# Stick-breaking attention: PSUM banks of the scores and of the transposed weights, three and two in place of two and three

## The chip, the cores and the metric

The kernel runs on one core of a Trainium2 chip. The metric is device time in microseconds, the median of several executions. The chip's engines are called as in the profile: PE (TensorE: PE for the matmuls, PEld for its weight loads), DVE (VectorE), ACT (ScalarE), POOL (GpSimd) and SP (SyncE, which here issues most of the transfers). Engines run on their own instruction streams, each in order, and wait for each other by semaphores. Matmuls write PSUM, which has eight banks of 128 x 512 float32; POOL works on SBUF alone in this kernel.

## The reference

One decoder layer over 2048 tokens of width 1024 with two groups of eight heads. Its parts: an adaptive RMS norm of x, one input projection, stick-breaking attention (group A, 64 wide), latent attention with a causal softmax (group B), gates, one output projection and a gated residual. The change is in group A alone:

```python
z = jnp.einsum('bhqd,bhkd->bhqk', qi, k).astype(jnp.float32) * inv_sqrt_d
strict = key_pos[None, :] < q_pos[:, None]
log_keep = jnp.where(strict, jax.nn.log_sigmoid(-z), 0.0)
after = lax.cumsum(log_keep, axis=3, reverse=True) - log_keep
w = jnp.where(strict, jnp.exp(jax.nn.log_sigmoid(z) + after), 0.0)
return jnp.einsum('bhqk,bhkd->bhqd', w.astype(v.dtype), v)
```

In words: each key takes a share of the stick that the later keys have left, so that the weight of a key is the difference of two neighbouring running products of sigmoid(-z), taken from the last key down.

## The kernel before

The kernel has five stages, one after the other: `features` and `tokens` (norm and projections), `attend_sb` (group A), `attend_mla` (group B) and `output`. The stage of group A runs from 836 us to 1320 us of the profiled execution, and the diff touches only it.

**Units and turns.** The stage goes over four pairs of heads, and within a pair over head 0 and head 1. The program of one pair is written out as a list (class `Plan`): 80 units and 80 turns. It is run once as straight code and then three times as the body of a loop, on every engine (`pairs`). So there are 320 units and 320 turns in all; below they are numbered 0 to 319, and turn 157, for example, is turn 77 of the second pair.

- A *unit* is one tile of scores: 128 queries against up to 512 keys. PE makes it by two matmuls (high and low part of q) and a third with the mask where the diagonal lies in it (L1734, L1737), into one of the banks z. ACT takes sigmoid(-z) from the bank into one of four buffers kp (L1574; `KEEPS = 4`, so it waits until DVE has used the unit four back). DVE turns it into the running product by a scan (L1651) and writes the row w.
- A *turn* brings 128 keys of a group of up to four query blocks, already scanned, into the form that the product with the values needs. PE transposes up to four 128 x 128 tiles into one of the banks pt (L1763). Three turns of four are *pooled* (`x % 4` is 0, 1 or 2): ACT copies the bank to SBUF (wf, L1585), which frees the bank; POOL rounds it (wh, L1546) and takes the rest (wl, L1548). The fourth (`x % 4` is 3) is not: ACT writes wh from the bank (L1590), and DVE takes wl from the same bank (L1660), so the bank is free only when DVE has done that.
- The *product* of a turn is two matmuls with the values (L1778, L1779), three turns later on PE (`LAG = 3`). It waits until the turn's wl is there: from POOL for pooled turns, from DVE for the others.
- At the end of each group of turns ACT and DVE add up, gate and split the result (L1598, L1670, L1677, L1610, L1689).

**The order.** All engines follow the same list. PE issues unit n + 1 and then the slot of n, which holds mostly one turn, sometimes none or two; each turn is followed by the product of the turn three back:

```python
unit(it, 0)
for n in range(U):
    if n + 1 < U:
        unit(it, n + 1)
    slot(it, turns_after(n, start))
```

ACT and DVE go unit n, then the slot of n. The turns begin at slot 21 of the first pair, since a group's rows must be scanned before it is turned, and so run into the next pair: turns 57 to 79 of a pair stand in slots 0 to 21 of the next one, and after the fourth pair 23 of them are left (`plan.rest`).

**Banks.** Two banks z, three banks pt (`PTS = 3`), two po for the products and one, `beside`, that holds zeros for the scan: eight. Unit n goes to bank n % 2 and waits until ACT has read unit n - 2 (`reached(pe, s_keep, it * U + n - 1)`). Turn x goes to bank x % 3 and waits until the turn that last used the bank has left it (`bank_before`, `bank_free`): ACT's copy for a pooled one, DVE's subtraction for the other kind. Since 80 is not a multiple of 3, turns 0 and 1 of a pair come only two turns after the last users of their banks.

## Time and profile before

| | us |
|---|---|
| median of 3 runs (lowest, highest) | 2053.9 (2050.63, 2054.33) |
| the profiled execution | 2051.65 |
| its span | 2050.0 |
| stage of group A | 836 to 1320 |
| its first rounding on POOL, its last subtraction there | 861.9, 1316.6 |

Over the whole span PE is busy 92%, its weight loads 75%, DVE 60%, POOL 50% and ACT 46%, and the granted TensorE clock is 0.958 of full speed on average. These shares are means over five stages with different limits, so for this change they say little: the stage itself has to be read, and in it what each engine waits for. A row of the timeline gives start, duration, engine, line, operation and tiles, and in brackets how long the engine had been idle and what ended that. The chain of work that ended last lies in the output stage and doesn't reach back to this one.

### The profile page before, as it was taken

To read this page: it belongs to the slowest core of one execution; us is meant where nothing else is said; L and a number is where in the kernel's file an instruction comes from. 1 tells how busy PE (TensorE), PEld (TensorE's weight loads), DVE (VectorE), ACT (ScalarE), POOL (GpSimd) and SP (SyncE) were. 2 spreads that over 40 slices of the span, in tenths; PEclk is the share of its full clock that TensorE was granted. 3 is DMA by queue.
4 is the path that set the end of the run, shared out by engine and by line. 5 is a ranking of instruction groups with operands and counts; after the bars stand their busy time and mean duration, and the time that the engine had idled before them with its cause. 6 is when DMAs were issued, how large, how long until landed. Compare 5 with 4: busy or idle time off the path is not lost. (4 is left out here: it accounts for less than half of the span.)

```text
span 2050.0 us, 32093 instructions
## 1 busy us (share of the span) xinstructions
PE 1880.1 (92%) x9669; PEld 1537.6 (75%) x9669; DVE 1236.6 (60%) x1864; ACT 948.1 (46%) x1890; POOL 1031.3 (50%) x1044
## 2 busy tenths in 40 slices
PE   6899999979999996599998989599999999997998
PEld 2687888859999985377777777468788887875776
DVE  1642222134555555699989899378988889873110
ACT  1431111133333332377777767457777777771000
POOL 2510000002333343199998989757878778781212
PEclk9899999989999997799999999779999999998999
DMA  7497532334555553731618052244153542605564
GB/s 267 135 320 223 174 112 77 129 145 143 177 200 184 178 177 131 177 82 39 169 37 188 24 152 59 69 101 83 38 125 75 134 82 57 170 21 174 174 195 143
DMA packets 224767, 273.75 MB, mean 134 GB/s; under 512 B 13936, under 2 KB 161680, under 8 KB 219264
## 3 DMA queue, kind: packets, MB, share of 16 engines
q1 hardware_dynamic: 220736, 265.53, 45.5%
q10 hardware_dynamic: 3904, 6.82, 1.1%
q8 instruction: 44, 0.72, 0.2%
q14 instruction: 83, 0.68, 0.1%
HBM read 159.06 MB, written 109.05 MB: 131 GB/s over the span
## 5 line engine op out<-in xcount | busy, mean ns | idle before, releaser
L2039 POOL TENSOR_TENSOR mla_wl<-mla_w,mla_wh 128x512 fp32r<-128x512 f32 (+1 forms) x320 | 379.2, 1200 | 112.8 <-ACT mla_wh L2075 107.0
L1548 POOL TENSOR_TENSOR sb_wl<-sb_wf,sb_wh 128x512 fp32r<-128x512 f32 (+2 forms) x240 | 285.5, 1189 | 19.2
L1651 DVE TENSOR_TENSOR_SCAN sb_w<-sb_kp,sb_w,sb_beside 128x512 f32<-128x512 f32 x192 | 245.5, 1278 | 28.0 <-ACT sb_kp L1574 12.5
L2074 ACT ACTIVATE mla_w<-mla_zt 128x512 f32<-128x512 f32 (+1 forms) x320 | 170.9, 534 | 114.0 <-PE mla_zt L2225 57.2
L2116 DVE TENSOR_REDUCE mla_nmx<-mla_zn 128x1 f32<-128x512 f32 (+2 forms) x320 | 191.3, 600 | 6.0 <-PE mla_zn L2195 3.1
L602 PE MATMUL pt_po<-h_hi,pt_wh 128*128 128x512 f32 x448 | 177.2, 396 | 9.7 <-issue 6.8
L1574 ACT ACTIVATE sb_kp<-sb_z 128x512 f32<-128x512 f32 (+3 forms) x320 | 168.8, 531 | 32.4 <-PE sb_z L1737 12.2
L1585 ACT ACTIVATE sb_wf<-sb_pt 128x512 f32<-128x512 f32 (+2 forms) x240 | 133.3, 555 | 108.3 <-PE sb_pt L1763 105.4
L1763 PE MATMUL sb_pt<-sb_ident,sb_w 128*128 128x128 f32 x1088 | 175.7, 277 | 7.3 <-DVE sb_wl L1660 6.9
L604 PE MATMUL pt_po<-h_hi,pt_wl 128*128 128x512 f32 x448 | 179.2, 400 | 0.0
L603 PE MATMUL pt_po<-h_lo,pt_wh 128*128 128x512 f32 x448 | 177.6, 396 | 0.0
L1546 POOL CAST sb_wh<-sb_wf 128x512 fp32r<-128x512 f32 (+2 forms) x240 | 143.6, 599 | 57.0 <-ACT sb_wf L1585 52.3
L2075 ACT ACTIVATE mla_wh<-mla_zt 128x512 fp32r<-128x512 f32 (+1 forms) x320 | 169.1, 529 | 0.0
L1778 PE MATMUL sb_po<-sb_wh,values 128*128 128x512 f32 (+1 forms) x320 | 145.1, 453 | 20.1 <-POOL sb_wl L1548 19.6
L1734 PE MATMUL sb_z<-keys,q_hi 128*128 128x512 f32 (+3 forms) x320 | 129.9, 406 | 34.0 <-DMA q_lo<-qk_sb 19.5
L1763 PEld LDWEIGHTS sb_pt<-sb_ident,sb_w 128*128 128x128 f32 x1088 | 130.6, 142 | 40.1 <-DVE sb_wl L1660 13.9
L83 POOL MEMSET tk_ident<- 128x128 f32 x1 | 0.2, 204 | 306.3 <-POOLq L62 306.3
L2195 PE MATMUL mla_zn<-keys,q_hi 96*128 96x512 f32 (+2 forms) x320 | 129.1, 409 | 24.8 <-DVE mla_nmx L2116 12.9
L2381 PE MATMUL out_po<-out_wh,out_ms 128*128 128x512 f32 x512 | 137.9, 391 | 6.0 <-DMA out_ms<-mix_mla 6.0
L2142 DVE TENSOR_TENSOR mla_pa<-mla_pa,mla_w 128x512 f32<-128x512 f32 x168 | 116.8, 695 | 30.9 <-ACT mla_w L2074 27.4
L2225 PE MATMUL mla_zt<-q_hi,keys 97*128 97x512 f32 (+1 forms) x320 | 125.9, 393 | 0.1
L2241 PE MATMUL mla_po<-mla_wh,values 128*128 128x512 f32 (+1 forms) x320 | 123.8, 387 | 1.4 <-POOL mla_wl L2039 1.4
(241 smaller groups left out, 4371.6 us busy)
## 6 DMA issues: line engine op xcount, KB each, us to landing
qk_mla<-tk_th SPq DMA_DIRECT2D x64, 192.0 KB, 2.1
qk_mla<-tk_tl SPq DMA_DIRECT2D x64, 192.0 KB, 2.3
whole<-in_w_ada SPq DMA_DIRECT2D x4, 2048.0 KB, 18.5
pt_w<-in_w_feat SPq DMA_DIRECT2D x16, 512.0 KB, 6.0
qk_sb<-pt_oh SPq DMA_DIRECT2D x32, 256.0 KB, 3.4
qk_sb<-pt_ol SPq DMA_DIRECT2D x32, 256.0 KB, 4.1
hT<-h_hi SPq DMA_DIRECT2D x16, 512.0 KB, 5.1
hT<-h_lo SPq DMA_DIRECT2D x16, 512.0 KB, 6.2
```

What stands on the lines that cost most here:

```text
L602: nc.tensor.matmul(bank[:], wh[s][:, k, :], hh[:, k, cols_q], start=(k == 0), stop=False)
L603: nc.tensor.matmul(bank[:], wh[s][:, k, :], hl[:, k, cols_q], start=False, stop=False)
L604: mm = nc.tensor.matmul(bank[:], wl[s][:, k, :], hh[:, k, cols_q], start=False, stop=(k == KD - 1))
L1548: nc.gpsimd.tensor_tensor(wl[i][:, lo:GW], wf[i][:, lo:GW], wh[i][:, lo:GW].bitcast(F32), ALU.subtract).then_inc(s_plo, 1)
L1574: nc.scalar.activation(kp[n % KEEPS][:, 0:width], z[n % 2][:, 0:width], ACT.Sigmoid, scale=-SB_SCALE).then_inc(s_keep, 1)
L1651: nc.vector.tensor_tensor_scan(kept, keeps, beside[:, 0:b - a], 1.0 if u["n"] == 0 else w[u["g"]][:, u["r"], b:b + 1], ALU.mult, ALU.bypas ...
L1763: tp = nc.tensor.transpose(pt[x % PTS][:, r * P:(r + 1) * P], w[tn["g"]][:, r, tn["j"] * P:(tn["j"] + 1) * P], ident[:])
L1778: nc.tensor.matmul(out, vj, wh[x % RING][:, lo:GW], start=tn["first"], stop=False)
L2039: nc.gpsimd.tensor_tensor(wl[i][:, cols], w[i][:, cols], wh[i][:, cols].bitcast(F32), ALU.subtract).then_inc(s_lo, 1)
L2074: nc.scalar.activation(w[i][:, cols], zt[x % 2][:, cols], ACT.Exp).then_inc(s_w, 1)
L2075: nc.scalar.activation(wh[i][:, cols], zt[x % 2][:, cols], ACT.Exp).then_inc(s_wh, 1)
L2116: nc.vector.tensor_reduce(nmx[pc["n"] % 2][:, pc["r"], pc["c"]:pc["c"] + 1], zn[p % 2][:, 0:pc["width"]], AX.X, ALU.max, negate=True).then ...
```

## The change

The stage's eight PSUM banks are shared out anew: three for the scores (`ZS = 3`) and two for the transposed weights (`PTS = 2`). Unit n goes to bank n % 3 and waits for ACT's sigmoid of the last unit that used the bank: unit n - 3, and for units 0 and 1 of a pair the unit two before. Turn x goes to bank x % 2 and waits for turn x - 2. No instruction that computes or moves data is added or taken away, and no transfer is moved.

```diff
-    PTS = 3
+    PTS = 2
+    ZS = 3
...
-        z = [m.ps(f"z{i}", [P, GW]) for i in range(2)]
+        z = [m.ps(f"z{i}", [P, GW]) for i in range(ZS)]
...
-                nc.scalar.activation(kp[n % KEEPS][:, 0:width], z[n % 2][:, 0:width], ACT.Sigmoid,
+                nc.scalar.activation(kp[n % KEEPS][:, 0:width], z[n % ZS][:, 0:width], ACT.Sigmoid,
...
+            def scores_before(n):
+
+                return n - ZS if n >= ZS else max(y for y in range(U) if y % ZS == n % ZS) - U
+
...
-                reached(pe, s_keep, it * U + n - 1)
+                reached(pe, s_keep, it * U + scores_before(n) + 1)
                 q = slice(i * P, (i + 1) * P)
-                out = z[n % 2][:, 0:u["z"] - u["a"]]
+                out = z[n % ZS][:, 0:u["z"] - u["a"]]
```

## Rows read from the trace of the kernel before

**Rows 1.** Windows: us, busy of the five engines, granted clock, DMA share, GB/s

```profile
861.90:1317.30 455.40, 419.82 (x2434) 332.55 (x2432) 396.45 (x440) 323.59 (x663) 417.75 (x480) 0.99 0.36 88
```

**Rows 2.** Groups by line, 836 to 1320 us: busy, mean ns, idle before them and its releaser

```profile
L1548 POOL TENSOR_TENSOR sb_wl<-sb_wf,sb_wh 128x512 fp32r<-128x512 f32 (+2 forms) x240 | 285.5, 1189 | 19.2
...
L1546 POOL CAST sb_wh<-sb_wf 128x512 fp32r<-128x512 f32 (+2 forms) x240 | 143.6, 599 | 57.0 <-ACT sb_wf L1585 52.3 <-PE sb_po L1779 4.0
...
L1651 DVE TENSOR_TENSOR_SCAN sb_w<-sb_kp,sb_w,sb_beside 128x512 f32<-128x512 f32 x192 | 245.5, 1278 | 28.0 <-ACT sb_kp L1574 12.5
...
L1660 DVE SCALAR_TENSOR_TENSOR sb_wl<-sb_pt,sb_wh 128x512 fp32r<-128x512 f32 (+1 forms) x80 | 40.8, 510 | 24.1 <-ACT sb_wh L1590 24.1
```

**Rows 3.** Waits, 836 to 1320 us: us in total, times, longest us

```profile
PEld sb_z L1734 <- ACT sb_kp L1574: 43.1, 83, 1.2
...
PE sb_z L1734 <- ACT sb_kp L1574: 12.7, 29, 0.9
...
PEld sb_pt L1763 <- DVE sb_wl L1660: 13.9, 17, 1.9
...
PE sb_pt L1763 <- DVE sb_wl L1660: 6.9, 7, 1.5
...
POOL sb_wh L1546 <- ACT sb_wf L1585: 52.3, 25, 38.6
...
POOL sb_wh L1546 <- PE sb_po L1779: 4.0, 1, 4.0
```

**Rows 4.** Timeline of POOL: the first instruction of the loop's body, third and fourth pair

```profile
1089.76 0.61 POOL L1546 CAST sb_wh<-sb_wf 128x512 fp32r<-128x512 f32 x1 [3.97 <-PE sb_po L1779]
...
1205.94 0.61 POOL L1546 CAST sb_wh<-sb_wf 128x512 fp32r<-128x512 f32 x1 [3.95 <-ACT sb_wf L1585]
```

**Rows 5.** Timeline around turn 157 (PE 1080.54) and the subtraction of turn 155 (DVE)

```profile
1080.54 0.49 PE L1763 MATMUL sb_pt<-sb_ident,sb_w 128*128 128x128 f32 x3
...
1081.14 0.49 ACT L1585 ACTIVATE sb_wf<-sb_pt 128x384 f32<-128x384 f32 x1 [0.37 <-PE sb_pt L1763]
...
1082.65 0.50 POOL L1546 CAST sb_wh<-sb_wf 128x384 fp32r<-128x384 f32 x1
...
1082.88 0.27 DVE L1660 SCALAR_TENSOR_TENSOR sb_wl<-sb_pt,sb_wh 128x128 fp32r<-128x128 f32 x1
...
1083.21 0.44 PE L1763 MATMUL sb_pt<-sb_ident,sb_w 128*128 128x128 f32 x2 [1.47 <-DVE sb_wl L1660]
```

**Rows 6.** Timeline around turn 93 (PE 991.21) and the subtraction of turn 91 (DVE)

```profile
991.21 0.51 PE L1763 MATMUL sb_pt<-sb_ident,sb_w 128*128 128x128 f32 x3
...
993.32 0.67 DVE L1660 SCALAR_TENSOR_TENSOR sb_wl<-sb_pt,sb_wh 128x512 fp32r<-128x512 f32 x1
...
993.40 0.50 POOL L1546 CAST sb_wh<-sb_wf 128x384 fp32r<-128x384 f32 x1
...
995.22 0.40 POOL L1546 CAST sb_wh<-sb_wf 128x256 fp32r<-128x256 f32 x1 [0.23 <-ACT sb_wf L1585]
```

**Rows 7.** Timeline around turn 237 (PE 1196.73) and the subtraction of turn 235 (DVE)

```profile
1196.73 0.49 PE L1763 MATMUL sb_pt<-sb_ident,sb_w 128*128 128x128 f32 x3
...
1198.50 0.27 DVE L1660 SCALAR_TENSOR_TENSOR sb_wl<-sb_pt,sb_wh 128x128 fp32r<-128x128 f32 x1
...
1198.76 0.97 POOL L1546 CAST sb_wh<-sb_wf 128x384 fp32r<-128x384 f32 x1
```

**Rows 8.** Timeline around turn 5 (PE 867.38) and the subtraction of turn 3 (DVE)

```profile
867.38 0.60 PE L1763 MATMUL sb_pt<-sb_ident,sb_w 128*128 128x128 f32 x4
...
867.75 0.67 DVE L1660 SCALAR_TENSOR_TENSOR sb_wl<-sb_pt,sb_wh 128x512 fp32r<-128x512 f32 x1
```

**Rows 9.** Timeline, subtraction of turn 183 (DVE), turn 185 (PE), rounding of turn 188 (POOL)

```profile
1124.46 0.67 DVE L1660 SCALAR_TENSOR_TENSOR sb_wl<-sb_pt,sb_wh 128x512 fp32r<-128x512 f32 x1
...
1124.65 0.49 PE L1763 MATMUL sb_pt<-sb_ident,sb_w 128*128 128x128 f32 x3
...
1129.82 0.61 POOL L1546 CAST sb_wh<-sb_wf 128x512 fp32r<-128x512 f32 x1 [0.30 <-ACT sb_wf L1585]
```

## The prediction

> **What bounds the stage now.** First the windows and the groups by line for the stage of group A, to see which engine has no time to give. From POOL's first rounding to its last subtraction are 455.4 us, and POOL is busy 417.75 of them, 92% [rows 1]; PE stands at 420 and DVE at 396, so no engine is far behind, but PE's time is that of pipelined matmuls and holds much waiting beside it. POOL's two groups add up to 285.5 + 143.6 = 429.1 us, with small overlaps between them [rows 2]. Next the waits. PE's longest is the one for a score bank: 43.1 + 12.7 = 55.8 us in 112 times, behind ACT's sigmoid. The one for a bank pt behind DVE's subtraction is 13.9 + 6.9 = 20.8 us in 24 times. POOL waited 52.3 us for ACT, but 38.6 of that is its start before the first turn; what is left is 13.7 us in 24 times, and 4.0 us once for PE [rows 3]. Two of these are no waits for data: at the first instruction of the loop's body POOL stood 3.97 us in the third pair and 3.95 us in the fourth, although the named releasers are different ones each time [rows 4]. I read that as the price of going back to the head of the loop, and it is the same for either kernel. So while the turns run, POOL waits for others 13.7 + 4.0 - 3.97 - 3.95 = 9.8 us in all. That is the most that any arrangement of banks can give back here; to take time away from PE's score waits is not yet to take it from the stage.
>
> The second thing to see is where DVE stands. Its full scans take 1.28 us each [rows 2], and in the first part of each pair, where turns 57 to 79 of the pair before are done, it has no gaps and runs late: the subtraction of turn 155 comes at 1082.88, and PE has waited 1.47 us for it when it begins turn 158 at 1083.21 [rows 5]. The release itself costs 1083.21 - (1082.88 + 0.27) = 0.06 us.
>
> **The change part by part.** Every instruction stays as it is, with its duration; only two waits of PE move.
>
> *The score wait* now asks for the sigmoid of unit n - 3. The two engines that it lies between are ACT and PE, and nearly all of the 55.8 us go, since the units are over 1 us apart and the 112 waits are 0.5 us on average. But PE only comes earlier to its next wait. Behind a unit stands a turn, which meets the bank pt, and the product, which waits for POOL's subtraction of the turn three back. For the stage the gain counts only where POOL was idle, so it lies between 0 and 9.8 us. Much of the 9.8 lies right after DVE's late stretch or at the start of a pair, where ACT or DVE is late, and not PE's unit. What is left is of the kind of the 0.30 us before turn 188 [rows 9], where POOL waits for a turn that stands on PE behind a product and a unit. I take two such waits, 0.6 us, for each of four pairs: **-2.4 us**.
>
> *The wait for bank pt* now asks for turn x - 2. Where that turn is pooled, ACT's copy frees the bank early enough: it ended 1081.14 + 0.49 = 1081.63 for turn 157, and PE's next turn began 1.58 us after that [rows 5]. Where it is of the kind that DVE finishes (79 times: each turn with x % 4 = 1), it is another matter, because ACT's copy and then DVE's scans come before the subtraction. What queues behind the held turn on PE: its own product of the turn three back, the next unit of scores, the next turns. Who waits for these: ACT for its copy, POOL for ACT's copy, and DVE for the unit's sigmoid. For each pair I take the latest turn and ask when POOL could have it.
>
> - Turn 157 began at 1080.54; ACT's copy ended 1.09 us later. Its bank would have been free at 1083.15 + 0.06 = 1083.21, 2.67 us late. The copy then ends at 1084.30, and POOL's rounding, which began at 1082.65, starts 1.65 us later [rows 5].
> - Turn 93: free at 993.32 + 0.67 + 0.06 = 994.05 against 991.21, 2.84 us late. With the same 1.09 us the copy ends at 995.14, against POOL's 993.40: 1.74 us, less the 0.23 us that POOL was idle before its next tile anyway: 1.5 us [rows 5, 6].
> - Turn 237: free at 1198.83 against 1196.73, 2.1 us late; copy at 1199.92 against 1198.76: 1.16 us [rows 5, 7].
>
> The earlier late turns of the same stretch don't add up with these: DVE's scans go on without a gap, since their sigmoids lie ready, so DVE keeps its times and only the latest turn counts. After it POOL has no idle time in which to catch up until the next pair starts, and the restart of the loop comes after its last tile, whenever that ends. So a delay here stays. Sum 1.65 + 1.5 + 1.16 = 4.3; to each I add 0.2 us for the hand-over from ACT to POOL, an estimate between the 0.06 us of PE's release and the 0.3 us that POOL was idle before turn 188 [rows 5, 9]: **+4.9 us**.
>
> In the first pair turns 5, 9 and 13 are late too; turn 5 would wait until 868.42 + 0.06 and began at 867.38, so 1.1 us [rows 8]. DVE is in its late stretch, but POOL has just started and has tiles in hand: between 0 and 1.1, I take **+0.5 us**.
>
> In the second part of each pair the turns are little late. The worst is turn 185: 1124.46 + 0.67 + 0.06 = 1125.19 against 1124.65, 0.54 us. POOL has tiles in hand there, but PE has two turns in the next slot and comes late to turn 188, for which POOL already waited 0.30 us [rows 9]. Between 0 and 0.54 for each of four pairs; nearer the upper end, because that wait shows no slack: 0.4 each, **+1.6 us**.
>
> Sum: -2.4 + 4.9 + 0.5 + 1.6 = +4.6 us. The profiled execution took 2051.65 us, 2.25 less than the median of the runs; 2051.65 + 4.6 = 2056.25, which on the median's footing is 2053.9 + 4.6 = 2058.5 us.
>
> The Trainium skill speaks against this sum. Its page "Perfetto Trace Analysis" says under "Matmuls" that independent groups of matmuls should rotate through different banks so that the evacuation of one overlaps the next, and under "Optimization Strategy" that a gap repeated on the engine that should be saturated can mean too little PSUM. By that, 112 repeated waits of PE for two score banks call for the third bank, and the result is the first rival below. The trace agrees that the gap is there; whether PE is the engine that should be saturated is what it leaves open, with POOL at 92%.
>
> **The rivals.**
>
> *The third score bank pays (faster).* PE runs a unit ahead, reaches the turns with x % 4 = 1 no earlier than DVE frees them, and POOL never waits. For it: the score wait is PE's largest, over twice its wait for pt. Against it: POOL's whole idle time is 9.8 us, and the late turns above take some. Price: about 7 of the 9.8, with the late turns absorbed: 2047 us. It decides if the held turns reach POOL before its tiles in hand are used up, that is if a turn is late by under about 1 us everywhere.
>
> *Nothing to be measured.* PE catches up within a few slots, as its score waits are gone, and the delays of 1 to 2 us once in a pair are given back: -2 to +2, 2054 us. For it: about 0.5 us saved in every third unit is near what the held turns cost. Against it: POOL has nothing in which to catch up.
>
> *The held turns hold DVE up too (much slower).* Units of scores stand on PE behind the held turn. If their sigmoids come too late, DVE gets gaps, its next subtraction is later still, and the delays add up instead of overlapping. The full lateness would then be paid: 2.67 + 2.84 + 2.1 + 1.1 + 4 x 0.54 = 10.9 us, and more with the other late turns of each stretch: 2065 to 2070 us. It decides from the point where the lateness, 2 to 3 us, is more than the time for which sigmoids lie ready for DVE, which is at most four buffers of kp, some 4 us.
>
> **How the numbers follow.** The mechanism of the sum, +2 to +9 us, has 0.58; that the gain and the loss cancel 0.16; that the third bank pays 0.12; that the delays add up 0.14. Two tenths of a per cent, about what can be told from no change here, are 4.1 us. Of the likeliest case some 0.17 lie below that. So: faster 0.12, the same 0.16 + 0.17 = 0.33, slower 0.41 + 0.14 = 0.55. The range leaves out the greater part of the faster rival below and half of the slowest above: 2051 to 2067 us; the likeliest case's own is 2056 to 2063.
>
> **What the profile would show.** The waits of PE for sb_kp fall from 55.8 us to under 5, or the first step is wrong. Those for DVE's sb_wl before sb_pt rise from 20.8 to 40 to 65 us, and come at turns with x % 4 = 1. POOL's waits for ACT, beside its start and the loop's head, rise from 9.8 us by 3 to 7, most of it one wait of 1 to 2 us late in the first part of each pair; if they fall, the first rival is right. POOL's, DVE's and ACT's busy times stay within 1%. DVE's waits for sb_kp (12.5 us before the full scans [rows 2]) stay; if they double, the last rival is. The stage gets longer by about 5 us, and the other stages don't change. The prediction would be wrong if delays in a pair's first part were given back before its end, or if DVE's scans lost their backlog.

## The result, and the profile after

The changed kernel takes 2071.44 us (median of 4 runs, 2070.62 to 2074.17) where the kernel before takes 2054.07 us beside it (4 runs): +17.4 us, a ratio of 1.0091 with a 95% interval of 1.0073 to 1.0108. The forecast was 2058.5 us with a range to 2067: the direction is right, the size is not. The profiled execution took 2074.17 us.

The page of the changed kernel, its first lines and the busy times:

```profile
span 2072.5 us, 32093 instructions
...
PE 1879.8 (91%) x9669; PEld 1547.5 (75%) x9669; DVE 1236.4 (60%) x1864; ACT 945.8 (46%) x1890; POOL 1026.6 (50%) x1044
```

The window from POOL's first rounding to its last subtraction, changed kernel (columns as in [rows 1]):

```profile
861.60:1337.10 475.50, 414.94 (x2431) 339.37 (x2429) 395.71 (x442) 321.26 (x663) 414.76 (x480) 0.96 0.35 84
```

It is 475.5 us where it was 455.4 [rows 1], and POOL is no busier in it. The spans differ by 22.5 us; all but 2.4 us of that is idle time of the engine that had none to give, in this one stage. The waits say who it waited for; changed kernel, 836 to 1345 us:

```profile
POOL sb_wh L1547 <- ACT sb_wf L1586: 59.5, 29, 38.1
...
DVE sb_w L1652 <- ACT sb_kp L1575: 55.6, 49, 15.3
...
PEld sb_pt L1768 <- DVE sb_wl L1661: 33.3, 42, 2.9
...
PE sb_pt L1768 <- DVE sb_wl L1661: 21.7, 19, 2.5
...
POOL sb_wh L1547 <- issue: 16.0, 2, 8.2
...
PEld sb_z L1739 <- ACT sb_kp L1575: 8.9, 14, 1.2
...
PE sb_z L1739 <- ACT sb_kp L1575: 4.0, 8, 0.7
...
POOL sb_wh L1547 <- PE sb_po L1784: 4.1, 6, 1.4
```

The wait for DVE's subtraction rose from 20.8 to 55.0 us [rows 3], within the forecast 40 to 65. The score wait fell from 55.8 to 12.9 us, and not to the "under 5" of the forecast. POOL's waits beside its start and the loop's head rose from 9.8 to 25.5 us (59.5 - 38.1 for ACT and 4.1 for PE), where 3 to 7 us more were forecast. And two rows were not foreseen: POOL stood 16.0 us in two waits for nothing that the profile shows ("issue"), and DVE waited 55.6 us for ACT's sigmoids, 15.3 of it at its start, where it had waited 33.4 with 14.7 at the start. The second shows in the groups by line, changed kernel:

```profile
L1652 DVE TENSOR_TENSOR_SCAN sb_w<-sb_kp,sb_w,sb_beside 128x512 f32<-128x512 f32 x192 | 245.5, 1278 | 45.5 <-ACT sb_kp L1575 31.2
```

The duration is that of [rows 2], but the 12.5 us behind ACT have become 31.2. Most of that growth is not from held turns, though. The two longest waits are the scans right after the heads of the loop's body, where DVE stands for ACT, ACT for PE and PE for POOL:

```profile
1108.40 1.28 DVE L1652 TENSOR_TENSOR_SCAN sb_w<-sb_kp,sb_w,sb_beside 128x512 f32<-128x512 f32 x1 [5.63 <-ACT sb_kp L1575]
...
1231.64 1.28 DVE L1652 TENSOR_TENSOR_SCAN sb_w<-sb_kp,sb_w,sb_beside 128x512 f32<-128x512 f32 x1 [6.09 <-ACT sb_kp L1575]
```

With the short ones behind them they are 14.6 us. Without them and the start, DVE's waits for sigmoids are 25.7 us, against 18.4 in the kernel before (18.7, less 0.3 at the same places).

**Where the 20 us came in.** I set the starts of POOL's 240 roundings side by side, changed kernel minus kernel before. This is worked out from the two timelines:

```
turn                 0     4     8    68    76    80   108   144   148   156   160   224   228   236   240   318
us later          -0.3  -0.3  +3.1  +3.8  +3.8  +6.2  +6.5  +5.8  +8.5  +8.5 +12.4 +12.6 +15.3 +15.2 +19.5 +19.8
```

There are four steps of 2.3 to 3.4 us (after turns 5, 77, 145 and 225, that is, x = 5, 77, 65, 65) and two of about 4 us at the heads of the loop's body (turns 160 and 240). The stage grew by 20.0 us: 8.1 at the two heads, 11.9 elsewhere.

**A held turn, read closely.** Timeline of the changed kernel around turn 5:

```profile
868.58 0.67 DVE L1661 SCALAR_TENSOR_TENSOR sb_wl<-sb_pt,sb_wh 128x512 fp32r<-128x512 f32 x1
...
869.29 0.66 PE L1768 MATMUL sb_pt<-sb_ident,sb_w 128*128 128x128 f32 x4 [2.47 <-DVE sb_wl L1661]
...
869.99 0.60 ACT L1586 ACTIVATE sb_wf<-sb_pt 128x512 f32<-128x512 f32 x1 [3.28 <-PE sb_pt L1768]
...
870.49 0.59 ACT L1575 ACTIVATE sb_kp<-sb_z 128x512 f32<-128x512 f32 x1
...
870.78 0.61 POOL L1547 CAST sb_wh<-sb_wf 128x512 fp32r<-128x512 f32 x1 [1.41 <-ACT sb_wf L1586]
...
873.83 1.28 DVE L1652 TENSOR_TENSOR_SCAN sb_w<-sb_kp,sb_w,sb_beside 128x512 f32<-128x512 f32 x1 [0.38 <-ACT sb_kp L1575]
```

PE stands 2.47 us for DVE's subtraction, ACT 3.28 us for PE. The scores that ACT reads at 870.49 were done on PE by 866.83 (the matmul at 866.43 lasts 0.40), and the buffer kp that it writes was free at 867.27, when DVE ended the scan of the unit four back. So this sigmoid is 3.2 us late only because it stands behind the copy of turn 5 in ACT's list. DVE still had sigmoids in hand here; its first wait is the 0.38 us at 873.83. What comes later on DVE makes its next subtraction later, and the next turn with it. And PE, when it goes on, goes at half speed. The changed kernel's windows (us, PE, PEld, DVE, ACT, POOL busy, granted clock, DMA share, GB/s):

```profile
866.00:870.00 4.00, 1.53 (x9) 1.03 (x8) 3.90 (x4) 0.72 (x3) 3.21 (x4) 1.00 0.00 0
870.00:872.00 2.00, 2.00 (x11) 1.84 (x10) 1.78 (x3) 1.58 (x4) 1.14 (x2) 0.68 0.00 0
872.00:874.00 2.00, 2.00 (x9) 1.71 (x9) 1.62 (x3) 0.85 (x3) 1.92 (x3) 0.50 0.01 4
```

The granted clock is 1.00 (2.4 GHz) up to the stand and falls to 0.50 (1.2 GHz) behind it: (1 - 0.68) x 2 + (1 - 0.50) x 2 = 1.6 us of PE's time. It does the same for 3.4 us from 973, 1072 and 1195 us, behind the stands at the other three steps (1.93, 2.23 and 2.23 us), and for 10 us after each head. It does not behind two stands of 2.22 and 1.95 us, at turns 65 and 89. In the kernel before it doesn't fall at any of these turns; its falls in this stage, 3.4 us each, are at 1208, 1290 and 1307 us.

**A head of the loop, read closely.** POOL and SP, changed kernel:

```profile
1093.67 0.74 POOL L1549 TENSOR_TENSOR sb_wl<-sb_wf,sb_wh 128x256 fp32r<-128x256 f32 x1
1102.18 0.61 POOL L1547 CAST sb_wh<-sb_wf 128x512 fp32r<-128x512 f32 x1 [7.76 <-issue]
...
1091.88 1.21 SPq L1452 DMA_DIRECT2D keys<-qk_sb  x2
1093.29 1.11 SPq L1452 DMA_DIRECT2D q_hi<-qk_sb  x2
1094.58 1.11 SPq L1452 DMA_DIRECT2D q_lo<-qk_sb  x2
...
1225.42 0.61 POOL L1547 CAST sb_wh<-sb_wf 128x512 fp32r<-128x512 f32 x1 [8.22 <-issue]
```

and the same place in the kernel before:

```profile
1085.04 0.74 POOL L1548 TENSOR_TENSOR sb_wl<-sb_wf,sb_wh 128x256 fp32r<-128x256 f32 x1
...
1085.74 1.21 SPq L1451 DMA_DIRECT2D keys<-qk_sb  x2
```

Before, SP began to issue the six transfers of 256 KB with the next pair's keys and queries 0.04 us before POOL's last tile ended (1085.78), and POOL went on after 3.97 us [rows 4]. After, POOL's last tile ends 8.6 us later. SP issues only 6.1 us later, as its queue goes by DVE's results: in front of the six stands the store of the last group's output. That is 2.5 us ahead of POOL's end, and POOL stands 7.76 us. In that time two packets of the queue "instruction" move. The DMA view of the changed kernel, 1096.4 to 1097.4 and 1099.6 to 1100.2 us:

```profile
q14 instruction: 1, 0.01, 3.2%
...
q14 instruction: 1, 0.01, 5.7%
```

The first of them begins 2.5 us after POOL's last tile (1094.41), the second ends 5.95 us after it; before, these were 0.0 and 2.04 us. The length of the stand goes with the second. I took all sixteen heads of the eight kernels in which the six transfers are issued ahead of POOL's end and within some 3 us of it: the stands range from 3.95 to 8.62 us, but POOL goes on 1.68 to 1.94 us after the second packet's end in every one (1.82 and 1.76 in the changed kernel). I read this as POOL's program behind the jump being fetched through DMA engines that the transfers keep busy; whose program a packet carries, the trace doesn't say.

### The profile page after: what moved, and what is told of

Same layout as the page of the kernel before. It is cut to its first block and busy times, and to the rows that moved or that the text cites. A ratio compares the mean times of both kernels' runs of the same rounds, so it can differ in the third digit from the quotient of the medians.

```text
span 2072.5 us, 32093 instructions
## 1 busy us (share of the span) xinstructions
PE 1879.8 (91%) x9669; PEld 1547.5 (75%) x9669; DVE 1236.4 (60%) x1864; ACT 945.8 (46%) x1890; POOL 1026.6 (50%) x1044
## 5 line engine op out<-in xcount | busy, mean ns | idle before, releaser
L2044 POOL TENSOR_TENSOR mla_wl<-mla_w,mla_wh 128x512 fp32r<-128x512 f32 (+1 forms) x320 | 377.6, 1195 | 117.1 <-ACT mla_wh L2080 111.1
L1652 DVE TENSOR_TENSOR_SCAN sb_w<-sb_kp,sb_w,sb_beside 128x512 f32<-128x512 f32 x192 | 245.5, 1278 | 45.5 <-ACT sb_kp L1575 31.2
L1547 POOL CAST sb_wh<-sb_wf 128x512 fp32r<-128x512 f32 (+2 forms) x240 | 142.3, 593 | 79.6 <-ACT sb_wf L1586 59.5
L1739 PE MATMUL sb_z<-keys,q_hi 128*128 128x512 f32 (+3 forms) x320 | 124.7, 390 | 24.2 <-DMA q_lo<-qk_sb 20.1
## 6 DMA issues: line engine op xcount, KB each, us to landing
whole<-in_w_ada SPq DMA_DIRECT2D x4, 2048.0 KB, 18.4
```

The costliest lines, as they stand in the source:

```text
L1652: nc.vector.tensor_tensor_scan(kept, keeps, beside[:, 0:b - a], 1.0 if u["n"] == 0 else w[u["g"]][:, u["r"], b:b + 1], ALU.mult, ALU.bypas ...
L2044: nc.gpsimd.tensor_tensor(wl[i][:, cols], w[i][:, cols], wh[i][:, cols].bitcast(F32), ALU.subtract).then_inc(s_lo, 1)
```

## The experiments

The table sums up all runs but two: the median against that of the kernel before, measured beside it; the growth of the stage (first to last rounding of POOL, against 453.8 us before), the part of it at the two heads (against 3.97 + 3.95 us), and the rest. The last three are from one profiled execution each, which can lie some us beside the median of its kernel (2.7 above it for the change, 3.9 for the kernel before with all three edits), so they show where time goes and not small differences.

```
kernel                                  time            stage   heads    rest
the change                             +17.4            +20.0    +8.1   +11.9
two banks z, two pt                    +18.4            +19.6    +7.3   +12.3
change, ACT ahead                       +9.7            +10.6    +4.2    +6.5
change, late keys                       +6.9             +8.7    -3.5   +12.2
change, late keys, z two               +10.4            +11.3    -2.5   +13.8
change, late keys, ACT ahead            +4.5             +4.2    -1.9    +6.1
change, DVE first                       +7.5            +12.1    +6.6    +5.5
change, DVE first, late keys            +0.3             +2.9    -1.4    +4.3
change, DVE first, ACT, late keys       -5.6             -4.8    -3.3    -1.5
before, late keys                       -0.2             -0.6    -1.1    +0.5
before, DVE first                       +4.8             +6.0    +7.7    -1.7
before, DVE first, late keys            -7.4             -4.4    -2.5    -1.9
before, DVE first, ACT, late keys       -8.7             -5.4    -3.5    -1.9
before, early keys                     +22.8            +24.6    +8.7   +15.9
change, matmuls at 5, 69, 77           +16.2            +21.7    +7.3   +14.5
change, late keys, the same            +10.6            +11.6    -2.7   +14.2
change, late keys, at 5, 65, 77         +5.5             +8.8    -1.9   +10.7
```

**One half of the change alone.** The third score bank is taken back, the second bank pt is not.

```diff
-    ZS = 3
+    ZS = 2
```

> Half of the change alone: two banks for the transposed weights, two for the scores as before, one bank unused. Theory A (the loss comes from the turns held for DVE's subtraction, and from POOL reaching the head of its loop after the key transfers were started): the stage loses as much as in the full change, +17 to +23 us against the kernel before, since the third score bank gave nothing back. Rival B (the third score bank itself does harm, because PE runs ahead and disturbs ACT's order): clearly less, +5 to +12 us. Rival C (the third score bank gives back part of the loss): more than the full change, +25 us or above.

2072.32 us, 1.0094 [1.0077, 1.0111]. So the loss is that of the third bank pt, and the third score bank is worth about 1 us beside it (18.4 - 17.4), which is within the intervals, and 3.5 us with late keys:

> Two banks for each, with late key transfers: against the third experiment it shows what the third score bank is worth when nothing collides. Theory A (nothing, or under 2 us, since PE's time is not what the stage lacks): +6 to +9 us against the kernel before. Rival C (it gives back part of the loss): +10 us or more.

2064.53 us, 1.0048 [1.0031, 1.0065], +10.4 us, which is over the 6 to 9 expected and by the sign of rival C gives part of the loss back. Against 1.0039 [1.0024, 1.0053] with three banks z the intervals overlap, so the third score bank is worth between nothing and some 3.5 us.

**ACT ahead.** ACT takes the sigmoid of unit n + 1 before the slot of n, as PE does, so that the copy of a held turn has one sigmoid fewer behind it.

```diff
+                unit(it, 0)
                 for n in range(U):
-                    unit(it, n)
+                    if n + 1 < U:
+                        unit(it, n + 1)
                     slot(it, turns_after(n, start))
```

> The changed kernel with ACT's list in PE's order: the sigmoid of unit n + 1 stands before the turns of slot n. Theory A says that ACT stands at the held turn and so cannot give DVE its next sigmoid, which leaves gaps in DVE; with this order the sigmoid is done before. It expects DVE's waits for sb_kp in the stage to fall from 55.6 to 30 to 40 us and the held-turn part of the loss (about 11 of 19 us) to fall by 5 to 10 us: +9 to +14 us against the kernel before. Rival D (POOL alone is starved by late turns, DVE's gaps do not matter): no gain, since POOL's copies come later in ACT's list, +17 to +24 us.

2063.6 us, 1.0054 [1.0036, 1.0073]. The part outside the heads falls from 11.9 to 6.5 us although every turn still waits for the same subtraction, and the waits of DVE for sb_kp from 55.6 to 32.8 us (some 8 of these 23 us right after the heads). The other 4 us are the heads, 6.09 and 6.01 us.

**Late keys.** SP waits for POOL's second tile of the next pair before it issues the six transfers.

```diff
                     sp.wait_ge(s_z, it * U + U)
+                    sp.wait_ge(s_plo, (it + 1) * plan.pooled_to(T - 1) + 2)
                     sp.sem_inc(s_step, 1)
                     load_qk(it + 1, 1)
```

> The changed kernel, with SP's transfers of the next pair's keys and queries of head 1 started only after POOL has done its first two pooled turns of the next pair, that is after POOL went back to the head of its loop. Theory A (the fetch of POOL's next instructions stands behind these transfers, which makes the two restarts 7.8 and 8.2 us in place of 4.0): both restarts fall to 4 us or below, and the time by about 8 us, to +9 to +13 us against the kernel before. Rival E (the restart is longer because of the banks or of PE's lateness, not the transfers): restarts stay at 7 to 8 us and the time at +17 to +21 us.

2060.84 us, 1.0039 [1.0024, 1.0053]. POOL and SP of this kernel:

```profile
1094.71 0.74 POOL L1550 TENSOR_TENSOR sb_wl<-sb_wf,sb_wh 128x256 fp32r<-128x256 f32 x1
1097.59 0.61 POOL L1548 CAST sb_wh<-sb_wf 128x512 fp32r<-128x512 f32 x1 [2.14 <-PE sb_po L1785]
...
1101.71 1.21 SPq L1452 DMA_DIRECT2D keys<-qk_sb  x2
```

With no transfer in the way the head takes 2.14 and 2.26 us in place of 7.76 and 8.22, 11.6 us less, and the time falls by 17.4 - 6.9 = 10.5. The rest of the stage is as in the change, 12.2 against 11.9 us, so the two causes add up. Here DVE waits 39.7 us for sigmoids, 14.8 of it at the start: with the heads out of the way this is 24.9 us, against 18.7 in the kernel before. The same line in the kernel before:

> The kernel before, with the same late start of the key transfers as in the third experiment. If the fetch at POOL's loop head stands behind the transfers, the kernel before pays for it too, in part: its restarts of 3.97 and 3.95 us fall to the 2.1 to 2.3 us that the third experiment showed, and the time by 3 to 5 us, a ratio of 0.998 to 0.9985. If the kernel before escaped the collision altogether (rival), the restarts stay at 4 us and the time is the same. Together with the third experiment this gives the price of the held turns without the collision: third minus this one, expected 9 to 12 us.

2053.92 us, 0.9999 [0.9985, 1.0013], a miss: its heads fell only to 3.35 and 3.51 us, and the 1.1 us that this is worth can't be seen. The price of the held turns, the third experiment minus this one, is then 7.1 us by the medians (9.3 by the stages, although the heads of the third are 2.5 us shorter), less than the 9 to 12 expected. The traces show what else lengthens these heads. In front of the six transfers SP issues three others of 256 KB, two stores and a gate, and these stay where they were; kernel before with late keys, and below it the gate of the change with late keys:

```profile
1088.22 0.35 SPq L1461 DMA_DIRECT2D sb_gate<-gates  x1
1088.23 0.74 POOL L1549 TENSOR_TENSOR sb_wl<-sb_wf,sb_wh 128x256 fp32r<-128x256 f32 x1
...
1092.32 0.61 POOL L1547 CAST sb_wh<-sb_wf 128x512 fp32r<-128x512 f32 x1 [3.35 <-ACT sb_wf L1586]
```

```profile
1092.21 0.35 SPq L1462 DMA_DIRECT2D sb_gate<-gates  x1
```

The gate, the last of the three, is issued 0.75 us before POOL's last tile ends (1088.97) in the first, and 3.24 us before it (1095.45) in the second. Over the twenty heads of the ten kernels with late keys the stand goes with this time: 2.1 to 2.4 us where the gate is 3.2 to 3.3 us ahead, 2.5 to 2.8 at 2.5 to 2.8, 2.9 to 3.4 at 2.1 to 2.4, and 3.35 and 3.51 at 0.75 and 1.36. No run moves these three transfers by themselves. Both of ACT ahead and late keys:

> The changed kernel with both edits: late key transfers and ACT's list in PE's order. The collision is out of the way in both, so against the third experiment (+6.9 us over the kernel before) only the order of ACT counts. Theory A (ACT stands at the held turn, and DVE lacks its sigmoid): a further 3 to 7 us less, 0 to +4 us against the kernel before. Rival G (the second experiment gained only because it moved POOL's restart relative to the transfers, 6 us in place of 8): no change against the third experiment, +5 to +9 us.

2058.56 us, 1.0022 [1.0009, 1.0035]. By the medians this is only 2.4 us less than with late keys alone (+4.5, just over the 0 to 4 expected), and the intervals overlap; in the profiled executions the part outside the heads falls from 12.2 to 6.1 us, and 1.6 us of that come back at the heads.

**Early keys.** The reverse, in the kernel before: the transfers are moved up by hand, to where DVE has 19 units of the next pair scanned.

```diff
                     load_gate(it, g - 2)
-                if not last:
-                    sp.wait_ge(s_z, it * U + U)
-                    sp.sem_inc(s_step, 1)
-                    load_qk(it + 1, 1)
+                    if g == 3 and not last:
+                        sp.wait_ge(s_z, it * U + U)
+                        sp.wait_ge(s_scan, (it + 1) * U + 19)
+                        sp.sem_inc(s_step, 1)
+                        load_qk(it + 1, 1)
                 store(it, 1)
```

> The kernel before, with its own banks; only SP's transfers of the next pair's keys and queries of head 1 start about 2 to 3 us earlier, at DVE's scan of unit 19 of the next pair, so that they are under way when POOL comes to its loop head. Theory A (the fetch of POOL's instructions stands behind them): the restarts go from 4.0 to 7 to 8.6 us, and the time up by 6 to 9 us. Rival E (the banks or PE's lateness made the restart long): restarts stay at 4 us, and the time is the same within 2 us.

2078.31 us, 1.0116 [1.0096, 1.0137], far more than expected. The timelines of SP and POOL, and a wait of DVE:

```profile
1092.23 1.20 SPq L1451 DMA_DIRECT2D keys<-qk_sb  x2
...
1094.05 0.73 POOL L1549 TENSOR_TENSOR sb_wl<-sb_wf,sb_wh 128x256 fp32r<-128x256 f32 x1
1103.22 0.61 POOL L1547 CAST sb_wh<-sb_wf 128x512 fp32r<-128x512 f32 x1 [8.43 <-issue]
...
DVE sb_om L1678 <- DMA sb_gate<-gates: 26.5, 3, 9.1
```

With three banks pt, and transfers that start 2.6 us ahead of POOL's end, the head takes 8.43 us, and the other 8.22: the banks have no part in it, only the order of the two. That is 8.7 us. The other 15.9 I put down to what stood behind the six transfers in SP's queue now: a gate that DVE waited 26.5 us for in three times. No run takes the two apart.

**DVE first.** DVE takes the slot of n before unit n, so that the subtraction comes before up to one more scan.

```diff
                 for n in range(U):
-                    unit(it, n)
                     slot(it, turns_after(n, start))
+                    unit(it, n)
```

> The changed kernel with late key transfers, and DVE does the slot of n (its subtraction of a turn) ahead of the scan of unit n, in place of behind it. The subtraction then frees the bank up to one scan (1.28 us) earlier. Theory A (the lateness of that subtraction is what holds PE, ACT and through them DVE and POOL): against the third experiment 2 to 6 us less, +1 to +5 us over the kernel before. If DVE now stands idle for ACT's part of the turn while a scan could run (rival), the time is that of the third experiment or more, and DVE's waits for sb_wh rise from 24 us.

> The changed kernel with DVE's subtraction ahead of the scan, and the key transfers where the change has them. The eighth experiment, with late transfers, took the whole loss away. Theory A: the POOL's restart grew because POOL came to its loop head some 2.5 us late relative to the transfers; with the held turns shortened it comes earlier again, so the restarts are 3 to 6 us and the time is within 0 to +5 us of the kernel before. Rival (the late transfers carried the gain of the eighth experiment, and the two add up): about 7 us above the kernel before.

> The kernel before, two banks for the scores and three for the transposed weights, with DVE's subtraction ahead of the scan. If the order of DVE is good in itself, the kernel before gains too, 2 to 6 us, and the change is then still the slower of the two by what is left of the held turns. If it only mends what the change broke, no difference: its own waits for the bank behind DVE's subtraction are 20.8 us against 55.0 in the changed kernel.

> The kernel before with DVE's subtraction first and late key transfers. The tenth experiment, without the late transfers, took 4.8 us more than the kernel before, and its restarts were 8.0 and 7.6 us. Theory A: that was the collision, and without it the time is 2049 to 2052 us, less than the kernel before. Rival: the order of DVE costs time in itself, and it stays at 2056 us or more.

2054.42 us, 1.0002 [0.9988, 1.0015], in the change with late keys; 2061.67, 1.0035 [1.0022, 1.0048], in the change; 2058.93, 1.0017 [1.0004, 1.0031], in the kernel before; 2048.17, 0.9961 [0.9945, 0.9977], in the kernel before with late keys. The second and third missed what was expected: the restarts of the change didn't go to 3 to 6 us but were 8.62 and 5.96. The third is the telling one: three banks pt, no turn that waits for DVE's subtraction, 1.7 us gained outside the heads, and yet slower, since its heads take 8.03 and 7.63 us. Late keys give them back (2.60 and 2.80): 10.3 us at the heads, 12 us by the medians. A faster DVE triggers the transfers earlier. With late keys DVE first gains about as much in either kernel by the medians (6.6 and 7.2 us), so by itself it doesn't take away the cost of the split: 7.1 us without it and 7.7 with it.

**All three together.**

> The changed kernel with all three edits: DVE's subtraction ahead of the scan, ACT's list in PE's order, late key transfers. Is there something left of the held turns for ACT's order to give (the eighth experiment stood at the time of the kernel before)? Theory A: 0 to 3 us less than the eighth, so 2051 to 2054 us. Rival: ACT's order costs, since its copies for POOL come later behind the sigmoids, and the time rises to 2056 us or more.

> The kernel before with the three edits of the eleventh experiment (DVE's subtraction first, ACT's list in PE's order, late key transfers). Against the eleventh it compares the two bank splits where the held turns are short. If the third score bank is worth more than the third bank of the turns there: over 2050.5 us. If the turns' third bank is still worth more: under 2047 us. I expect the latter, 2044 to 2048 us, since e11 still waits 22.0 us for DVE's subtraction.

2048.57 us, 0.9972 [0.9961, 0.9984], with the change's banks, and 2046.85 us, 0.9957 [0.9943, 0.997], with those of before. Both beat both kernels. In this order the split of the banks costs 0.3 us outside the heads (-1.52 against -1.87), where it cost 11.9 in the order as it is, and 3.1 us by the medians: the turns are held about as little as in the kernel before (22.0 us against 20.8). It also gives the control for ACT ahead. Added to DVE first and late keys, it takes 5.8 us off in the change (4.3 to -1.5; 5.9 by the medians), and nothing outside the heads in the kernel before (-1.9 to -1.9; 1.3 us by the medians). So ACT's order is worth its 6 us only where turns are held. The waits of the first, 836 to 1345 us:

```profile
DVE sb_w L1655 <- ACT sb_kp L1576: 17.2, 6, 15.4
PEld sb_pt L1771 <- DVE sb_wl L1664: 14.1, 18, 1.9
...
PE sb_pt L1771 <- DVE sb_wl L1664: 7.9, 10, 1.7
```

Of the 17.2 us 15.4 are DVE's start. Which of the two splits is better here stays open, as the intervals overlap.

**The clock.** Twelve matmuls of constants, 1.45 us, go in front of turns that PE stands at, into the score bank of the unit after next. They are meant to leave the stand as long as it is and only fill it; nothing that is used later is changed.

```diff
+            def fill(it, n):
+
+                reached(pe, s_keep, it * U + scores_before(n) + 1)
+                for _ in range(FILL):
+                    nc.tensor.matmul(z[n % ZS][:, 0:P], identr[:], maskr[:], start=True, stop=True)
...
                 for x, back in turns:
+                    if n is not None and (x in (65, 77) or (x == 5 and isinstance(it, int) and it == 0 and not back)):
+                        fill(it, n + 2)
                     turn(it - back, x)
```

> The changed kernel, with twelve matmuls of 128 columns between two constants put in front of turn 5 of the first pair and turns 69 and 77 of each pair, into the score bank of the unit after next, whose next unit overwrites it. They lie inside the time for which PE stands at these turns (2.5, 2.2 and 1.9 us in the changed kernel). Nothing that is read later is changed. Theory 'the clock': PE's long stand at these turns is followed by a granted clock of 0.5 for some 4 us (870 to 874, 972 to 978, 1072 to 1076, 1194 to 1200 us), 1.7 us of PE's time lost each time, and it is there that the delay against the kernel before jumps by 2.3 to 3.1 us; with the matmuls in place the clock stays at 1.0 there and the kernel gets faster than the changed one by 3 to 6 us: +11 to +14 us over the kernel before. Theory 'ACT's order alone': the length of the stand is all that counts, the clock is a bystander: the clock stays up and the time does not fall: +16 to +20 us. If the matmuls last longer than the stand, up to 1 us is lost at each of nine places.

> The same twelve matmuls in the changed kernel whose key and query transfers wait for POOL's last tile of the pair (+6.9 us over the kernel before without the matmuls, five falls of the clock in the stage, 1.7 us each). Theory 'the clock': four of the five falls go and with them 3 to 6 us: +1 to +4 us over the kernel before. Theory 'ACT's order alone': +6 to +9 us.

> The changed kernel with the late key and query transfers and with the twelve matmuls of constants in front of turn 5 of the first pair and turns 65 and 77 of each pair. In the traces so far the long stands before turn 5 (2.5 us), turn 65 of every pair (2.2 us) and turn 77 of the first pair (1.9 us) are followed by a granted clock of 0.5 and 1.7 us of PE's time are lost each time; with the matmuls the falls at turns 5 and 77 went, and the delay up to turn 8 grew by 1.6 us in place of 3.1 us, but turn 65 had none, and there the falls stayed. Theory 'the clock': four falls (870, 954, 1074, 1190 us) go, about 1.6 us less each, so that the stage grows between the loops' heads by 5 to 8 us in place of 12.2, and the kernel is at 0 to +4 us over the kernel before (+6.9 without the matmuls). Theory 'the stand alone': the falls go and the time stays, +6 to +9 us. If the matmuls cost as much as they bring, because turns come behind them that would not have been held, the falls go at turn 65 and the delay after it is the same as without them, 2.7 us.

In the first two the matmuls stood in front of 69, which hardly waits, in place of 65 (the 2.2 us that the first expectation names are turn 65's), and they gave 2071.08 us, 1.0084 [1.007, 1.0098], and 2065.48 us, 1.0048 [1.0036, 1.0061]: nothing gained, and the second slower than without the matmuls. The third gave 2061.05 us, 1.0032 [1.0019, 1.0044]. Its windows at turn 145, and below them the row of the same stand without the matmuls:

```profile
1072.00:1074.00 2.00, 1.58 (x10) 1.36 (x11) 2.00 (x3) 0.92 (x2) 0.96 (x2) 1.00 0.00 0
1074.00:1076.00 2.00, 2.00 (x14) 1.69 (x14) 1.79 (x3) 1.21 (x4) 1.84 (x4) 1.00 0.84 260
1076.00:1078.00 2.00, 1.75 (x12) 1.31 (x12) 2.00 (x3) 1.13 (x3) 1.42 (x3) 1.00 0.50 137
```

```profile
1074.00:1076.00 2.00, 2.00 (x10) 1.52 (x9) 1.90 (x3) 1.29 (x3) 1.26 (x2) 0.68 0.42 155
1076.00:1078.00 2.00, 2.00 (x8) 1.61 (x8) 1.90 (x4) 0.77 (x2) 1.33 (x3) 0.50 0.81 212
```

The clock stays at 1.00, and four of five falls are gone; the one at turn 89 stays, and one comes in at 1318 us, near the stage's end. The step after turn 145 is 1.2 us in place of 2.8. The changed kernel agrees: its stand of 2.22 us at turn 65, without a fall, is followed by a step of 1.1 us, those of 2.23 us at turns 145 and 225, with one, by steps of 2.7. But the growth outside the heads is 10.7 against 12.2 us, 1.5 us less (a growth of 5 to 8 was expected), and the medians, +5.5 and +6.9 us, have intervals that overlap. What one stand no longer loses, a later one mostly does: between turns 80 and 89 the delay grows by 2.4 us with the matmuls and by 1.0 without. The kernel with two banks of each says the same from the other side: it has one fall outside the heads' stretches before 1300 us, and its rest is 12.3 us, as large as that of the change with four. The falls are a small part of the cost, and my theory that they are much of it fell.

**Three banks of each.** The zeros of the scan move from PSUM to SBUF, which frees the eighth bank.

```diff
-    PTS = 2
+    PTS = 3
...
-        beside = m.ps("beside", [P, GW])
+        beside = m.sb("beside", [P, GW])
```

> Three banks for the scores and three for the transposed weights; the eighth bank comes from the zeros of DVE's scan, which move to SBUF (contents are the same). It gives the third score bank its full chance without taking one from the turns. My sum gave that -2.4 us; its bound from POOL's idle time was -9.8 us. Theory A: 0 to -5 us against the kernel before. Rival F (the score wait of 55.8 us was a limit of the stage): -10 us or more. If DVE's scan with two inputs from SBUF gets slower or blocks POOL, the time rises by over 5 us and POOL's durations show it; then this run says nothing on the banks alone.

> The kernel before with the zeros of DVE's scan in SBUF in place of PSUM, nothing else: the control for the fourth experiment, which had this and a third score bank and took 207 us more. If the two SBUF inputs of the scan are the whole cause, the same +200 to +215 us, with POOL's rounding at 1.1 us in place of 0.6 and full scans at 1.6 us in place of 1.28. The difference to the fourth is what a third score bank is worth beside three banks for the turns, when POOL and DVE block each other: under 5 us by theory A.

2261.58 us, 1.1022 [1.1002, 1.1043]; the second, which only moves the zeros in the kernel before, 2260.44 us, 1.1002 [1.0983, 1.102]. So all of it is the zeros. Groups by line of the second, from 836 us:

```profile
L1548 POOL TENSOR_TENSOR sb_wl<-sb_wf,sb_wh 128x512 fp32r<-128x512 f32 (+2 forms) x240 | 366.2, 1526 | 19.2
L1651 DVE TENSOR_TENSOR_SCAN sb_w<-sb_kp,sb_w,sb_beside 128x512 f32<-128x512 f32 x192 | 318.1, 1657 | 88.3 <-ACT sb_kp L1574 77.3
L1546 POOL CAST sb_wh<-sb_wf 128x512 fp32r<-128x512 f32 (+2 forms) x240 | 269.8, 1124 | 58.7 <-ACT sb_wf L1585 43.4 <-issue 15.1 <-PE sb_po L1779 0.2
```

POOL's two groups grew by 80.7 + 126.2 = 206.9 us against [rows 2], and the kernel by 206.3: POOL is what bounds this stage, and a us more on it is a us more in all. (DVE's full scans grew too, by 72.6 us; it is POOL's sum that matches.) The Trainium skill, "SBUF — State Buffer", section "Who interferes with whom", says that a VectorE instruction with two SBUF inputs contends with a GpSimd instruction that reads SBUF. The trace agrees: both POOL's groups and the scan, which went from 1.28 to 1.66 us, are longer.

## Why the forecast was off

- *What bounds the stage* held. POOL bounds it (the 206.9 us above), and the 55.8 us of score waits were not worth their length. The Trainium skill's rule that independent groups of matmuls should rotate through different PSUM banks ("Perfetto Trace Analysis", "Matmuls") points at this gap and gives no price: 42.9 us of score waits went, and the bank brought between nothing and 3.5 us. The forecast had 2.4. Its sign for this step, score waits under 5 us, did not come: 12.9 are left.
- *The held turns* were right as a mechanism: the wait for DVE's subtraction rose to 55.0 us, within the 40 to 65 forecast. Their size was forecast at 4.9 + 0.5 + 1.6 = 7.0 us, and with the third bank's 2.4 taken off at 4.6; the stage shows 11.9 with the bank's gain in it. **The step that failed** is "DVE's scans go on without a gap, since their sigmoids lie ready, so DVE keeps its times and only the latest turn counts". The latest turns (157, 93, 237) show little; the steps came at 5, 77, 145 and 225. The sigmoids don't lie ready: the one behind turn 5 came 3.2 us late. The rival of delays that add up named this, with 10.9 us and a sign to look for, a doubling of the waits for sb_kp. That they more than doubled (12.5 to 31.2 us) is in the main the heads' doing, 14.1 of the 18.7 us; with the heads out of the way they grow from 18.7 to 24.9 us in all. And the rival had mostly the wrong queue: it is ACT's list in which the sigmoid stands behind the copy of the held turn, and seldom PE's, in which the unit does (at 873.20 ACT waits 0.94 us for it). That the reorder of ACT alone takes 5.4 to 6.1 us off outside the heads (11.9 to 6.5, 12.2 to 6.1), that with DVE's it takes off nearly all, and that it brings nothing there with three banks pt, shows that the delay runs through ACT's order. How the rest divides between the stand itself and the clock is shown only in part: 1.5 us for four of the five falls, from one execution each.
- *The loop's head*, "the same for either kernel", was **the other step that failed**, and the only one that the rivals had not in them: the heads grew by 8.1 us in the profile. (Late keys took 11.6 us off them, 10.5 by the medians, since they shorten the stands below those of the kernel before.) Both rows were at hand: SP's transfers at 1085.74 and POOL's end at 1085.78, at the start of a collision. I had read the 3.97 and 3.95 us as a constant from two instances that shared that accident.
- *Sum:* 7.0 - 2.4 forecast, 11.9 (the bank's gain within it) + 8.1 = 20.0 us in the profiled execution. That execution took 2.7 us more than its median, and the medians differ by 17.4. *Busy times within 1%* held (POOL 414.8 against 417.8 in the window), and the other stages kept their length but for 2.4 us.
- *Open:* whether three banks z are worth anything in the best order. That late keys don't bring the heads of the kernel before to 2.1 us, as they do in the change, goes with how close the gate's transfer lies, but no run moves that one. That the "instruction" packets carry POOL's program is argued from their times, not shown; that the transfers lengthen the head is shown, by moving them both ways.

## What to carry to other kernels

Before a bank is given to the engine with the longest wait, ask which engine has no idle time, and what stands behind the wait that the lost bank creates in every in-order list: a copy that waits holds up the next sigmoid too. A fixed-looking cost at the head of a loop is fixed only as long as the transfers beside it start when they did; look at what releases them, and hold them back by a semaphore if they are not urgent. When a reorder doesn't pay, look for what it triggered: DVE first was measured at +4.8 us, and at -7.4 once the keys were held back, which by itself brought 0.2.

## What the hardware showed that I had not expected

- POOL's stand at the head of the loop's body goes with how long before its last tile's end the six transfers of 256 KB begin to be issued: 3.97 and 3.95 us with 0.04 and 0.66 us, 6.0 to 6.1 with 1.4 to 1.6 us, and 7.4 to 8.6 with 1.7 to 3.2 us (sixteen heads of eight kernels, among them both splits of the banks). With the six held back it is 2.1 to 3.5 us (twenty heads of ten kernels), mostly the shorter the longer ago the transfer in front of them was issued.
- In those sixteen heads POOL went on 1.68 to 1.94 us after the end of the second 8 KB packet of the queue "instruction", whatever the length of the stand.
- The granted TensorE clock fell from 2.4 to 1.2 GHz for 3.4 us behind four stands of PE of 1.93 to 2.47 us in the middle of a busy stage, and not behind two others of 1.95 and 2.22 us. Half of 3.4, 1.7 us, is what PE's work in it loses each time at most. With matmuls placed within the stands it stayed at 2.4 GHz behind four of five, and the time fell by no more than the intervals of the runs.
- A scan with its second input in SBUF in place of PSUM slowed POOL's cast from 0.60 to 1.12 us and its subtraction from 1.19 to 1.53 us, 10% of the whole kernel.
